# The second block's mixer in another order: stick scores among the projection tiles, value columns last

## What is computed

```python
proj = h @ w_in[i]
sb_q, sb_k, sb_v, q_lat, kv_lat, k_rope = jnp.split(proj, split_at, axis=-1)
# stick breaking, per head (64 wide), strict = key before query
z = q @ k.T * scale
log_keep = where(strict, -softplus(z), 0)
log_keep_after = reverse_cumsum(log_keep) - log_keep
weights = where(strict, exp(log_sigmoid(z) + log_keep_after), 0);  o_sb = weights @ v
# latent attention
q = rms_norm_2(q_lat) @ w_q_up;   kv = rms_norm_2(kv_lat) @ w_kv_up     # 256 and 128 wide inputs
q_rope, k_rope = apply_rope(...)
o_mla = softmax(causal(q_nope @ k_nope.T + q_rope @ k_rope.T) * scale) @ v
mix = concat([rms_norm_2(o_sb), rms_norm_2(o_mla)]) @ w_o
```

## Time and profile before

| what | value |
|---|---|
| median of 3 runs | 1144.12 us (1143.04 to 1152.59) |
| profiled execution, span of its instructions | 1159.4 us |
| the mixer in it, first dense tile to `o` | 732.34 to 874.76 us |
| of it: last 13 projection tiles | 742.78 to 780.29 |
| from there to the first `mla` score | 780.29 to 843.07 |
| `mla` to its last output product | 843.07 to 867.60 |
| from there to `o` | 867.60 to 874.76 |

### The profile page before, as it was taken

One profiled execution on the slowest core, in us unless ns is written; L12 is line 12 of the kernel. 1 busy time (PEld: TensorE's weight loads), 2 busy tenths in 40 slices (PEclk: granted clock), 3 DMA queues, 4 the chain that ended last, 5 costly groups with the idle time before them and its releaser, 6 DMA issues.

```text
span 1159.4 us, 17499 instructions
## 1 busy us (share of the span) xinstructions
PE 1054.3 (91%) x6662; PEld 943.0 (81%) x6662; DVE 809.9 (70%) x1571; ACT 614.7 (53%) x1143; POOL 185.2 (16%) x86
## 2 busy tenths in 40 slices
PE   4997699999999797879999999999889899999976
PEld 4996478888889796768888888996568799999865
DVE  4799778967868635676776667656554678777775
ACT  5552276654646545454665464455444466645555
POOL 1682002122121000001121221120000000010210
PEclk9996689999999896689999999997779899999988
DMA  8442024555554331102455554530122255554511
GB/s 344 148 178 76 1 80 175 214 183 184 183 181 177 115 131 57 37 1 76 179 194 203 182 185 177 187 119 1 36 109 73 109 181 183 170 194 173 187 41 37
DMA packets 22834, 158.28 MB, mean 137 GB/s; under 512 B 2528, under 2 KB 2784, under 8 KB 4448
## 3 DMA queue, kind: packets, MB, share of 16 engines
q1 hardware_dynamic: 21888, 153.51, 36.9%
q10 hardware_dynamic: 864, 3.66, 0.8%
HBM read 156.12 MB, written 1.05 MB: 136 GB/s over the span
## 4 chain that ended last, share of the span: by engine, by line
PE 75%; DVE 18%; ACT 4%; issue 2%; DMA 1%; DVEq 0%; ACTq 0%
PE bank L685 72%; DVE obank L1903 5%; PE obank L685 2%; DVE split_lo L578 1%; PE bank L817 1%; DVE square_sum L1895 1%; DVE temps L1895 1%; DVE probs L1899 1%; DVE mlp_parts L1903 1%; DMA consts<-in_consts 1%; ACT L1324 1%; DVE rowmax L2404 1%; ACT act_parts L1327 1%; DVE x L1895 1%; ACT split_hi L570 1%
## 5 line engine op out<-in xcount | busy, mean ns | idle before, releaser
L685 PE MATMUL bank<-act_parts,split_hi 128*128 128x256 f32 (+1 forms) x1632 | 340.7, 306 | 30.6 <-DVE split_lo L578 13.1
L570 ACT ACTIVATE split_hi<-ring 128x1024 fp32r<-128x1024 f32 (+1 forms) x280 | 289.9, 1049 | 133.0 <-PE bank L685 131.6
L578 POOL TENSOR_TENSOR split_lo<-ring,split_hi 128x1024 fp32r<-128x1024 f32 (+1 forms) x74 | 181.8, 2461 | 936.5 <-ACT split_hi L570 936.5
L685 PEld LDWEIGHTS bank<-act_parts,split_hi 128*128 128x128 f32 x1632 | 270.3, 200 | 42.4 <-issue 26.2
L578 DVE TENSOR_TENSOR split_lo<-ring,split_hi 128x1024 fp32r<-128x1024 f32 (+1 forms) x206 | 248.7, 1217 | 40.3 <-ACT split_hi L570 39.4
L685 PE MATMUL bank<-hidden_parts,split_hi 128*128 128x512 f32 (+1 forms) x816 | 265.8, 378 | 0.8 <-DVE hidden_parts L1903 0.8
L685 PE MATMUL bank<-act_parts,split_lo 128*128 128x256 f32 x880 | 256.2, 291 | 0.0
L685 PE MATMUL bank<-hidden_parts,split_lo 128*128 128x256 f32 x752 | 211.8, 282 | 0.0
L685 PE MATMUL bank<-mlp_parts,split_hi 128*128 128x512 f32 x512 | 181.8, 400 | 2.3 <-DVE mlp_parts L1903 2.3
L685 PEld LDWEIGHTS bank<-act_parts,split_lo 128*128 128x128 f32 x880 | 176.8, 201 | 0.0
L685 PEld LDWEIGHTS bank<-hidden_parts,split_hi 128*128 128x128 f32 x816 | 149.0, 188 | 31.8 <-DVE hidden_parts L1903 1.0
(11 more groups left out here) (255 smaller groups left out, 1347.8 us busy)
## 6 DMA issues: line engine op xcount, KB each, us to landing
ring<-in_weights SPq DMA_DIRECT2D x141, 1024.0 KB, 4.8
ring<-in_weights SPq DMA_DIRECT2D x5, 768.0 KB, 4.1
x<-in_x ACTq DMA_DIRECT2D x1, 1024.0 KB, 7.8
y<-in_mem ACTq DMA_DIRECT2D x1, 1024.0 KB, 9.8
out<-x SPq DMA_DIRECT2D x4, 256.0 KB, 2.5
consts<-in_consts ACTq DMA_DIRECT2D x1, 885.0 KB, 12.8
ring<-in_weights SPq DMA_DIRECT2D x1, 512.0 KB, 3.6
consts<-in_consts ACTq DMA_DIRECT2D x1, 260.0 KB, 7.8
```

Of the source, the lines that this page charges most:

```text
L570: nc.scalar.activation(split_hi[:, w % SPLIT, 0:n], src, ACT.Copy).then_inc(sem("high_parts"), 1)
L578: (nc.vector if engine == "vector" else nc.gpsimd).tensor_tensor(split_lo[:, w % SPLIT, 0:n], src, split_hi[:, w % SPLIT, 0:n].bitcast(F32 ...
L685: return nc.tensor.matmul(dst, lhsT, rhs, start=start, stop=stop)
```

## The change

1. The weight columns are ordered anew: `s_in` has 10 tiles, stick query and key tiles in turn (q0, k0, q1, k1, ...), then the 2 of query latent; `s_lat` as before; the 4 value tiles come last as `s_val`.
2. PE issues a pair of scores after the two tiles of their heads, between dense tiles; then 4 sums, the latent tiles and their statistics, and the value tiles in four pieces (a pair of tiles for one half of the tokens each) with norms, `q_up`, sums and swaps between. All 8 stick outputs come after `v_up`.
3. The sticks' statistic and broadcast, and DVE's and ACT's work on them, move into `mla`.
4. `o` begins with the first four steps (the stick half) of its first four tiles, ahead of the transposes of `mla`'s output; the second halves follow them, waiting step by step. The 8 products that keep PE busy go.
5. The rope angles (13 DVE instructions) and their sine and cosine move into the second MLP of the first block. Every second split of the later projection tiles goes to POOL. Scores lie in other buffers.

```diff
+        "s_in": cols(*pairs, s[:, 1536:1792]), "s_lat": krope, "s_val": s[:, 1024:1536],
+        beside_sticks = w % 2 == 1 and (stage in ("s_lat", "s_val") or (stage == "s_in" and t >= SPLIT))
```

PE's program:

```diff
+            normed("smix", "s_in", projected)
+            linear("s_in", 3, 2, projected)
+            stick_scores(0)
+            stick_scores(1)
+            linear("s_in", 5, 1, projected)
+            stick_scores(2)
+            stick_scores(3)
+            linear("s_in", 6, 1, projected)
+            for t in range(7, 10):
+                stick_scores(t - 3)
+                linear("s_in", t, 1, projected)
+            stick_scores(7)
+            pe.wait_ge(sem("sb.below"), 1)
             for h in range(4):
                 stick_sums(h)
+            linear("s_lat", 0, 1, projected)
+            full_stat("qlat", 2, signal=1)
+            linear("s_lat", 1, 1, projected)
+            full_stat("kvlat", 1, src=sq[:, 2:3, :], signal=1)
+            linear_tokens("s_val", 0, 2, projected, (0,))
+            full_bcast("qlat")
+            full_bcast("kvlat")
...
+            linear_tokens("s_val", 0, 2, projected, (1,))
+            query_heads(range(4))
             for h in range(4, 8):
                 stick_sums(h)
+            linear_tokens("s_val", 2, 2, projected, (0,))
+            query_swaps(range(2))
+            query_heads(range(4, 6))
+            linear_tokens("s_val", 2, 2, projected, (1,))
+            query_heads(range(6, 8))
...
+            query_swaps(range(2, 4))
...
+            for h in range(8):
+                stick_outputs(h)
...
+                if w == 1:
+                    full_stat("sb", 4)
+                if w == 3:
+                    full_bcast("sb")
...
+            for t in range(SPLIT):
+                output_blocks(t, 0)
             for tt in range(TT):
                 pe.wait_ge(sem("mla.o"), tt + 1)
...
-            keep_busy(take("o", 0), 8)
-            pe.wait_ge(sem("o.act"), 2)
-            linear("o", 0, KD, projected)
+            for t in range(SPLIT):
+                output_blocks(t, 4)
+            linear("o", SPLIT, KD - SPLIT, projected)
```

ACT's program (DVE's is interleaved in the same manner):

```diff
+            stick_decays(range(2))
+            pump("s_in", 5)
+            stick_decays(range(2, 4))
+            pump("s_in", 6)
+            stick_logs(range(4))
+            pump("s_in", 7)
+            stick_decays(range(4, 6))
...
+            stick_weights(range(4))
+            for t in range(2):
+                wait_emptied(act, "s_in", 8 + t)
+            do(flat(sq[:, 0:2, :]), flat(lat[:, 0:2, :]), ACT.Square).then_inc(sem("qlat.squares"), 1)
+            stick_logs(range(4, 8))
+            pump("s_lat", 0)
+            wait_emptied(act, "s_lat", 0)
+            do(sq[:, 2, :], lat[:, 2, :], ACT.Square).then_inc(sem("kvlat.squares"), 1)
+            pump("s_lat", 1)
+            root("qlat", 2, 256)
+            root("kvlat", 2, 128)
...
+            exponentials("mla", range(2))
             load_root()
             stick_squares(range(4))
             root("sb", 2, 512)
+            exponentials("mla", range(2, 4))
```

More of the change, by code:

```diff
@@ L1191, in _ @@
             mlp_block(1)
[L1193 to L1204, removed]
             def stick_scores(h):
+                for t in (h - h % 2, h - h % 2 + 1):
+                    wait_emptied(pe, "s_in", t)
                 dst = take("sb.Z", h)
@@ L1246, in query_heads, with query_swaps @@
                     ready(last)
-            wait_emptied(pe, "qlat.bc", 0)
-            for h in range(6):
-                stick_scores(h)
-            query_heads(range(4))
+            def query_swaps(pairs):
+                for j in pairs:
+                    wait_emptied(pe, "q_up", 2 * j)
+                    wait_emptied(pe, "q_up", 2 * j + 1)
+                    dst = take("q.swap", j)
+                    for i in range(2):
+                        last = mm(dst[0:96, SEQ * i:SEQ * i + SEQ], const("swap")[64:96, :], qcat[64:96, 2 * j + i, :])
+                    ready(last)
@@ L1282, in _, with output_blocks @@
             wait_emptied(pe, "k_up", 7)
-            wait_emptied(pe, "v_up", 0)
-            wait_emptied(pe, "v_up", 1)
-            attention("mla")
+            units = UNITS["mla"]
+            scores("mla", units[0], 0)
+            for w in range(len(units) + 2):
+                if w + 1 < len(units):
+                    scores("mla", units[w + 1], w + 1)
+                if 1 <= w <= len(units):
+                    probs_transposed("mla", units[w - 1], w - 1)
+                if w == 1:
+                    full_stat("sb", 4)
+                if w == 3:
+                    full_bcast("sb")
+                if w == 2:
+                    wait_emptied(pe, "v_up", 0)
+                    wait_emptied(pe, "v_up", 1)
+                if w >= 2:
+                    outputs("mla", units[w - 2], w - 2)
+            def output_blocks(t, first):
+                w, _ = split_tile("o", t)
+                dst = take("o", t) if first == 0 else bank("o", t)
+                for k in range(first, first + 4):
+                    if t == 0 and first:
+                        pe.wait_ge(sem("o.act"), k - 2)
+                    last = product(dst[:, 0:SEQ], [part[:, k, :] for part in w], [part[:, k, :] for part in projected],
+                                   k == 0, k == KD - 1)
+                if first:
+                    ready(last)
+            pe.wait_ge(sem("o.act"), 1)
+            for t in range(SPLIT):
+                output_blocks(t, 0)
             for tt in range(TT):
@@ L1739, in _ @@
             root("sb", 2, 512)
-            for h in range(8):
-                empty(("k_up", h), kcat[0:64, h, :], bank("k_up", h)[0:64, 0:SEQ])
+            exponentials("mla", range(2, 4))
             wait_emptied(act, "sb.bc", 0)
             high(flat(act_hi[:, 0:4, :]), flat(mix[:, 0:4, :]), "sb.high")
-            exponentials("mla")
+            exponentials("mla", range(4, 6))
             for tt in range(TT):
@@ L1752, in _ @@
                 wait_emptied(act, "mla.oT", tt)
-            high(flat(act_hi[:, 4:8, :]), flat(mix[:, 4:8, :]), "mla.high")
+            for t in range(4, 8):
+                high(act_hi[:, t, :], mix[:, t, :], "mla.high")
             def raw_outputs(stage, norm, gname):
@@ L2581, in _, with rotated @@
-            invert("sb", 2)
-            for j in range(4):
+            def rotated(j):
                 heads = slice(2 * j, 2 * j + 2)
```

346 lines of the change are left out of this document (187 added, 159 removed).

## The result

The change takes the median from 1152.01 us (20 runs, 1142.04 to 1158.93) to **1141.74 us** (20 runs, 1135.96 to 1150.93). The ratio is **0.994, 95% interval 0.9918 to 0.9963**. In a second comparison, with 12 and 23 runs, it was 0.993 [0.9893, 0.9968]. So the kernel is faster, by 0.4 to 0.8% in the first and 0.3 to 1.1% in the second. The forecast of 1126 us (1114 to 1138) is missed: the time is 3.7 us above the range. The saving is 10.3 us by the medians and 7.8 by the means (1149.8 and 1142.0), where 18.1 were expected. The ratios compare fast runs only, so two of the 23 runs of before, more than 1.5% above the fastest, are left out of the second, and by the same measure the profiled execution of before, about 1161 us (its span of 1159.4 and the 1.8 us that lie between span and time in the changed kernel's profiled run), is a slow one.

What follows compares the result with a forecast made beforehand. PE's waits and the 1.2 GHz clock level were taken to bound the mixer. Terms -19.2 (stretch), +3.5 (`mla`) and -2.4 (tail) sum to -18.1 us, off the 1144.1 median: 1126 us, range 1114 to 1138.

Steps and rivals of the forecast that it cites:

- What bounds the kernel: Whole mixer: PE's order and waits decide; 94.5 us hold two kinds of loss, waits and the 1.2 GHz level.
- The stretch: Fourth projection tile to first `mla` score: 74.1 us of work at 2.4 GHz plus waits and one fall; 19.2 us earlier.
- The waits: Latent statistics, first value piece and later banks, between projections and `mla`: 1.1, 0.7, 2.0 and 1.2, together 5.0 us.
- The one fall of the clock at that place: Around the kv statistic and first value piece, 782.4 to 785.7: one clock fall costing 2.0 us, bounds 0 and 5.
- the hand-offs between DVE and ACT: Rival for the head groups: DVE and ACT set the pace, both groups 5 us late, 1136 us; chance 0.15.
- the clock was not lost at the scores: Rival at the first scores: clock falls and stays low, 34 us lost, 1160 us; chance 0.04.
- `mla`: First score to last output: a 4.1 us wait for the sticks' statistic, then low clock; 28 us, 3.5 later.
- From the span to the forecast: Whole kernel: 18.1 us saved in the 1159.4 us profiled span, taken off the 1144.1 median, gives 1126 us.
- The tail: Last `mla` output through `o`: half tiles fill the wait, 4.0 us gained less 1.6 for low clock; 2.4 us earlier.
- The 1.6 us that the forecast set aside for half tiles at the low clock: Start of `o`: first half tiles begin at the low clock, taking 1.6 us from a 4.0 us gain.
- The MLP: Second MLP of the first block: angles and a sine table load fit into free DVE and ACT time, costing nothing.
- one of the prediction's own signs of being wrong: In the profile after, MLP gaps behind the angles would show the forecast wrong; no size given.

Runs made afterwards that it cites:

- the three repetitions: The kernel before, unchanged, profiled three more times: 1153.76, 1145.96 and 1143.34 us.
- its own experiment: The kernel before with only `o` begun in half tiles, splits in pieces and no products to keep PE busy: 1147.22 us, ratio 0.999.

## Why the prediction was wrong, step by step

**What bounds the kernel: right.** Waits and the 1.2 GHz level were the two losses. Of the 20 us that the stretch became shorter, about 4 are idle time (means 6.6 and 2.7) and about 2 the products of the sticks' statistic, which left the stretch (1.95 us in the run that put them back); most of the rest is clock. Length times twice the shortfall of the clock gives 27 to 40 us at the low level in the four executions of before, and 0 to 3 in the three of the changed kernel.

**The stretch: right.** First sums were forecast for 772.0 and stand at 771.72; the first `mla` score for 823.9, at 820.87. The waits: none before the query statistic (1.1 forecast), 0.30 before the kv one (0.7), 2.01 before the first value piece (2.0), 0.17 later (1.2). The one fall of the clock at that place came and passed within a few tiles. Mean saving 20.3 us by three profiles against four, forecast 19.2.

No rival took the place of this: the hand-offs between DVE and ACT held nothing up by more than those waits, and the clock was not lost at the scores. One reading in the prediction was wrong without changing the sum: from 804 to 818 PE waited three times, each time for a part (`keep_lo`), and not for a bank. What the Trainium skill says in "TensorE: Matmul & The Clock Gate" (A second HAM failure mode: psum-queue depth-cycling), that cycling through banks with short idles between can make the clock swing, is not borne out by this stretch, which went through a bank for each tile, score and sum at a mean of 0.98 with 2.5 us of idle time. Nor is it refuted: the clock did fall once, briefly, behind the 2.01 us wait (a single wait, for a bank), and for 13 us behind the 4.07 us one.

**`mla`: the step that failed.** The forecast was "24.53 us, mostly at 1.2 GHz" becoming 28, "3.5 us later". The mechanism was as written: exponentials, table load and squares give a wait of 4.07 us (4.1 forecast), and the clock is 0.50 behind it. And 28 was near the three measured (27.37, 29.68, 33.70; mean 30.3). The base was off. The 24.53 of the earlier trace rows is one outcome of a gap after which the clock falls in some executions and not in others; three other executions took 18.25 to 19.86. With a mean of 20.6 the change costs 9.6 us here instead of 3.5, and 10.9 against the three repetitions alone (mean 19.3). The 24.53 is no matter of that one execution either: it came again in the kernel before with PE kept busy. The experiments show the cost from both sides: with the statistic ahead of it `mla` takes 20.93, and with PE busy in the wait 25.74.

**From the span to the forecast: the second failure.** "That span is 15 us above the median of the runs, 1144.1; the saving is one of absolute time" took a saving worked out against an unusually long execution off a median of three runs that was itself low: two of the three fell in the group near 1144, and with 17 more the median was 1152.01. In the profiled pair the forecast held: span 1141 forecast, 1139.6 measured. That is in part luck, since it compares with the execution whose `mla` was long. Off the median of 20 runs, 1152.0, the same saving gives 1134.

**The tail: right.** Forecast 2.4, measured 2.5 (means 31.08 and 28.60), and shown alone by its own experiment. The 1.6 us that the forecast set aside for half tiles at the low clock show too: in the three runs where the granted clock of this tail was 1.00 it took 27.12, 1.5 less.

**The MLP: wrong, small.** "In 20 us PE is never idle while DVE has 7 and ACT 6 us free" was true as an average and no cover: DVE works in the order of its program, the angle steps stand in it ahead of the split of the next weight tile, and beside POOL's splits one step took 2.44 us and one weight split 3.38, so that two tiles came 0.98 and 1.17 us late. Priced at 0, it cost 2.6. A gap behind the angles was one of the prediction's own signs of being wrong. In the mixer too an instruction of DVE is long beside a POOL split (2.71 us at 782.60 for a `decays` step of 0.55), but there PE waited for none of it.

**The sum of it.** Forecast 1126, measured 1141.7, so 15.7 us too low: base 7.9 (1152.0 - 1144.1), `mla` 6.1, MLP 2.6, stretch -1.1, tail -0.1, together 15.4. The measured stages of the profiles give -20.3 + 9.6 - 2.5 + 2.6 = -10.6 us, and without the execution shown -8.7; the medians differ by 10.3, the means by 7.8. Differences of 3 us between these can't be settled with seven profiles, those of before spread over 18 us.

## What to carry to other kernels

Before a saving is worked out from a stage, look at that stage in more than one execution, above all where a gap stands in it after which the clock may or may not fall: a wait's price is its length plus a fall that differs from execution to execution. Moving an operation out of a poor stage pays only if its inputs are ready at its new place; here one statistic moved back ahead of the first score was worth 5.9 us in a pair of profiles. And free time of an engine on average covers nothing if the added work stands, in that engine's order, ahead of what the critical engine will ask for next, above all where a neighbour engine's work can make one of its instructions several times longer.

## What the hardware showed that was not expected

- In a row of six 64-row scores the granted clock fell although PE had waited only 0.23 us ahead of them (steps of 1.1 us for two, then 1.85, then the slow row at 781.52), while two pairs and four single ones between dense tiles kept 1.00.
- The same 2.23 us gap was followed by transposes of 1.11 us in one execution and of 0.65 in another. Behind the 2.01 us wait for the first value piece the clock fell in one execution of the changed kernel (0.50 from 786 to 788) and stayed at 1.00 through the whole stretch in another (78.61 us long).
- Once down behind the 4.07 us wait, the clock stayed at 0.50 with PE fully busy for about 7, 13 and 28 us in three executions of the same kernel (`mla` 27.37, 29.68 and 33.70 us, the last one into the tail). Behind the 2.01 us wait it came back within 4 us, with a value piece on PE.
- Beside a POOL weight split (2.4 us), a DVE step of 0.29 us took 2.44 and a DVE weight split of 1.22 took 3.38.
- The executions of a program on one core fall in two groups, before near 1144 and near 1152 us; the clock from 380 to 540 us is 0.86 in the one and 0.83 in the other, and the mixer starts 5 to 8 us later at 0.83.
